# A decoder block with 16,384 experts: first routing result in two halves, row buffers moved, two gathers asked for one stage earlier

## The reference, cut to what matters

```
h = layer_norm(DN_ALPHA * h + merged @ w_out, ln1_g, ln1_b)
q = (h @ w_q).reshape(n, 8, 2, 128)                 # 8 heads, two halves of a key
s = einsum('nhpc,pkc->nhpk', q, sub_keys)           # 128 scores for each half
sv, si = top_k(s, 16)
cand = sv[:, :, 0, :, None] + sv[:, :, 1, None, :]  # 16 x 16 candidates
top_s, pos = top_k(cand, 16)
experts = take_along_axis(cand_idx, pos)            # 16 of 16384 experts for each token and head
gates = softmax(top_s)
act = gelu(einsum('nd,nhkd->nhk', x, u_table[experts])) * gates
out = einsum('nhk,nhkd->nd', act, v_table[experts])
h = layer_norm(DN_ALPHA * h + out, ln2_g, ln2_b)
```

## Time and profile before

| | |
|---|---|
| median of 3 runs | 2435.24 us (2434.62 to 2436.1) |
| the profiled execution, its own time | 2436.59 us |
| its span, first to last instruction | 2434.8 us |
| PE busy | 2155.4 us, 89% |
| DVE busy | 1532.0 us, 63% |
| indirect gathers (queue q0) | 537.01 MB, 52.5% of the 16 DMA engines' span |

### The profile page before, as it was taken

One profiled execution on the slowest core, in us unless ns is written; L12 is line 12 of the kernel. 1 busy time (PEld: TensorE's weight loads), 2 busy tenths in 40 slices (PEclk: granted clock), 3 DMA queues, 4 the chain that ended last, 5 costly groups with the idle time before them and its releaser, 6 DMA issues.

```text
span 2434.8 us, 37735 instructions
## 1 busy us (share of the span) xinstructions
PE 2155.4 (89%) x15287; PEld 1510.0 (62%) x15287; DVE 1532.0 (63%) x2592; ACT 676.3 (28%) x1353; POOL 669.1 (27%) x538
## 2 busy tenths in 40 slices
PE   7999999999999999998988989978887787777776
PEld 6999999999899999887544444433332333222232
DVE  7778888888765454448765576667445544444445
ACT  4555555455344444433111111111111000000000
POOL 1000000000000000003644554555455445444542
PEclk9999999999999999999999999999999999999999
DMA  5433333333366666666999999999999999999997
GB/s 201 130 104 101 105 87 101 104 92 92 102 198 191 184 186 186 210 224 243 416 417 424 420 427 427 427 427 427 427 427 428 426 427 427 427 427 427 427 427 285
DMA packets 346273, 708.19 MB, mean 291 GB/s; under 512 B 13835, under 2 KB 270435, under 8 KB 279779
## 3 DMA queue, kind: packets, MB, share of 16 engines
q0 software_dynamic: 74176, 537.01, 52.5%
q1 hardware_dynamic: 271684, 168.55, 23.4%
q10 hardware_dynamic: 240, 0.22, 0.0%
HBM read 703.63 MB, written 2.10 MB: 290 GB/s over the span
## 4 chain that ended last, share of the span: by engine, by line
DMA 35%; PE 12%; DVE 3%; issue 2%; POOL 1%; DVEq 1%; ACT 0%; POOLq 0%; ACTq 0%
DMA down_rows<-in_v_table,experts 28%; DMA up_rows<-in_u_table,experts 7%; PE bank L1782 7%; PE project L1782 3%; PE bank L1698 1%; DVE up_rows L1898 1%; POOL down_rows L1686 1%; PE bank L1740 0%; PE bank L1725 0%; PE bank L1746 0%; ACT diagonal L1842 0%; DVE one_hot L1348 0%; DVE expert_sides L1354 0%; POOL up_rows L1680 0%; DVE side_index L1327 0%
## 5 line engine op out<-in xcount | busy, mean ns | idle before, releaser
L1898 DVE CUSTOM_DVE_ANT_0 up_rows<-up_rows,h 128x2048 f32<-128x2048 f32 x256 | 585.3, 2292 | 525.9 <-DMA up_rows<-in_u_table,experts 525.8
L1782 PE MATMUL bank<-down_rows,diagonal 128*128 128x512 f32 x1520 | 709.7, 604 | 141.5 <-DMA down_rows<-in_v_table,experts 109.0
L1782 PEld LDWEIGHTS bank<-down_rows,diagonal 128*128 128x128 f32 x1520 | 282.0, 192 | 551.3 <-issue 310.5
L1680 POOL DMA_INDIRECT up_rows<-in_u_table,experts x256 | 286.2, 1118 | 1169.8 <-POOLq L1366 1055.9
L1686 POOL DMA_INDIRECT down_rows<-in_v_table,experts x256 | 374.7, 1464 | 522.5 <-PE bank L1782 508.6
L192 DVE TENSOR_TENSOR w_half_rest<-w_half,w_half_high 128x1024 fp32r<-128x1024 f32 x224 | 271.3, 1219 | 160.1 <-ACT w_half_high L171 159.9
L207 PE MATMUL project<-hT_high,w_half_high 128*128 128x272 f32 (+1 forms) x1152 | 351.5, 305 | 0.4 <-PEq L214 0.3
L207 PE MATMUL project<-hT,w_half_high 128*128 128x272 f32 (+1 forms) x1152 | 329.7, 286 | 0.0
L207 PE MATMUL project<-hT_high,w_half_rest 128*128 128x272 f32 (+1 forms) x1152 | 329.2, 286 | 0.0
L1782 PE MATMUL project<-down_rows,diagonal 128*128 128x512 f32 x512 | 258.8, 629 | 75.6 <-DMA down_rows<-in_v_table,experts 70.6
L171 ACT CAST w_half_high<-w_half 128x1024 fp32r<-128x1024 f32 x224 | 234.7, 1050 | 205.2 <-PE merge_ps L207 121.0
(11 more groups left out here) (376 smaller groups left out, 3043.5 us busy)
## 6 DMA issues: line engine op xcount, KB each, us to landing
w_half<-in_w_in SPq DMA_DIRECT2D x176, 512.0 KB, 3.9
w_half<-in_w_branch_a SPq DMA_DIRECT2D x32, 512.0 KB, 3.8
out_w<-in_w_out SPq DMA_DIRECT2D x16, 1024.0 KB, 5.3
query_w<-in_w_q_peer SPq DMA_DIRECT2D x10, 1024.0 KB, 24.9
w_half<-in_w_branch_b SPq DMA_DIRECT2D x16, 512.0 KB, 3.8
out_w<-in_w_q_peer SPq DMA_DIRECT2D x6, 1024.0 KB, 36.2
up_rows<-in_u_table,experts POOLq DMA_INDIRECT x256, 21.1
down_rows<-in_v_table,experts POOLq DMA_INDIRECT x256, 20.5
```

The source lines that it names most:

```text
L1680: pool.indirect_dma_start(ur[n % RU], None, w["u_table"][0], bass.IndirectOffsetOnAxis(ap=k.idx[:, t, h, j:j + 1], axis=0)).then_inc(s_u[n ...
L1782: mm = nc.tensor.matmul(acc[t][c][:], dg[n % RD][:], vr[n % RV][:, quarter(c)], start=(n == 0), stop=(n == last(t, c)), skip_group_check=True)
L1898: v.tensor_tensor_reduce(ur[n % RU], ur[n % RU], k.h[:, n // (HEADS * TOPK), :], 1.0, 0.0, ALU.mult, ALU.add, dots[:, n:n + 1]).then_inc(s ...
```

## The change

Four things are done at once.

1. In the output stage DVE's order changes: the evacuations and statistics of block n now stand behind the rest bits of quarter 4n + 5; before, they stood behind those of quarter 4n + 6. The loads of head 0's query weights go from g = 4 and 5 to g = 5 and 6.
2. The first routing takes its 16 experts in two halves of 8, and signals `s_ahead` after the first.
3. At the end of the output stage POOL waits for `s_ahead` (and `s_free`, that PE is done with the buffers which lie in the same place) and issues up rows 0 and 1 there. For this the row buffers are allocated earlier: up rows 0, 1, 4, 5 and down rows 0, 1 share the place of six weight buffers of the output stage, up rows 2 and 3 take the place that down rows 3 and 4 had. Before, nine of the eleven buffers started at multiples of 512 bytes and two at bytes 35,520 and 43,712. Now the six start at 130,944 + 8192 i, two at 35,520 and 43,712, and the last three at 180,160, 188,352 and 196,544.
4. After up row 5, POOL issues down rows 0 to 4 in one go; up rows 8 to 15 wait for the second half's `s_idx`.

```diff
+RU, EARLY = 6, 2
...
+    def up_row(self, n):
+        i = n % RU
+        if i in (2, 3):
+            return self.down_or_up[i - 2]
+        return self.rows[:, i if i < 2 else i - 2, :]
...
+def experts(k, h, t, j):
...
+    v.tensor_scalar(k.pij[:, 0, j], k.ti[:, j], 4, None, ALU.logical_shift_right)
+    v.tensor_scalar(k.pij[:, 1, j], k.ti[:, j], 15, None, ALU.bitwise_and)
...
+    return v.tensor_copy(k.idx[:, t, h, j], ex)
...
+    flat, best, rest = cand[:].rearrange("p a b -> p (a b)"), slice(0, 8), slice(8, 16)
+    if halves:
+        v.max(tv[:, best], flat)
+        d()
+        v.max_index(ti[:, best], tv[:, best], flat)
+        v.match_replace(k.cand2[:], tv[:, best], flat, -3.0e38)
+        d()
+        experts(k, h, t, best).then_inc(k.s_ahead, 1)
+        v.max(tv[:, rest], k.cand2[:])
+        d()
+        v.max_index(ti[:, rest], tv[:, rest], k.cand2[:])
+        v.tensor_tensor(k.gates[:, t, h, :], tv[:], tv[:, 0:1].to_broadcast((P, TOPK)), ALU.subtract).then_inc(k.s_shift, 1)
+        d()
+        experts(k, h, t, rest).then_inc(k.s_idx, 1)
+        return
...
-                if g in (4, 5):
-                    k.load_query(sp, w, 0, g - 4)
+                if g in (5, 6):
+                    k.load_query(sp, w, 0, g - 5)
...
-            part(last, 0, 1, 3)
+            part(last, 0, 1, 3).then_inc(k.s_free, 1)
...
-            for g in range(2, 7):
-                rest(g)
             for n in range(NB - 1):
+                for g in range(4 * n + 2, 4 * n + 6):
+                    rest(g)
                 for t in range(TT):
                     evacuate(n, t)
...
-                for g in range(4 * n + 7, min(4 * n + 11, QUARTERS)):
-                    rest(g)
+            for g in range(4 * NB - 2, QUARTERS):
+                rest(g)
             first_tile()
-            route(k, dve, 0, 0)
+            route(k, dve, 0, 0, halves=True)
+
+        @block.gpsimd
+        def _(pool):
+            pool.wait_ge(k.s_ahead, 1)
+            pool.wait_ge(k.s_free, 1)
+            for n in range(EARLY):
+                k.load_up(pool, w, n)
...
-                        if j == 0:
+                        if n == TOPK // 2:
+                            pool.wait_ge(s_idx, 1)
+                        if n and j == 0:
                             pool.wait_ge(s_idx, 2 * h + t + 1)
...
+                        k.load_up(pool, w, n)
+                        if n == RU - 1:
+                            for m in range(RV):
+                                down(m)
```

More of the change, by code:

```diff
@@ L139, in open_routing @@
         self.qT = [self.sb(f"queryT{i}", [P, SEQ]) for i in range(2)]
+        self.rows_at = self.next_at()
+        self.rows = self.sb("rows", [P, 6, D])
+        self.down_or_up = [self.over(f"up_rows{2 + i}", [P, D], self.hT_high_at + 4 * D * i)[:] for i in range(2)]
+        self.s_up, self.s_ahead, self.s_free = [self.sem(f"up_arrived{i}") for i in range(RU)], self.sem("route_idx_first"), self.sem("out_first_free")
         self.s_query_w, self.s_gb = [self.sem(f"query_w{i}") for i in range(3)], self.sem("ln1_gamma_beta")
@@ L1328, in best16, with route @@
     v.drain()
-def route(k, dve, h, t):
+def experts(k, h, t, j):
+    v, d, n = k.nc.vector, k.nc.vector.drain, j.stop - j.start
+    pf, hot, ef, ex = k.pf[:, :, j], k.hot[:, :, j, :], k.ef[:, :, j], k.ex[:, j]
+    v.tensor_scalar(k.pij[:, 0, j], k.ti[:, j], 4, None, ALU.logical_shift_right)
+    v.tensor_scalar(k.pij[:, 1, j], k.ti[:, j], 15, None, ALU.bitwise_and)
+    d()
+    v.tensor_copy(pf, k.pij[:, :, j])
+    d()
+    for i in range(2):
+        v.tensor_tensor(hot[:, i], pf[:, i].rearrange("p (n a) -> p n a", a=1).to_broadcast((P, n, TOPK)),
+                        k.kept[:, C_IOTA:C_IOTA + TOPK].rearrange("p (a n) -> p a n", a=1).to_broadcast((P, n, TOPK)), ALU.is_equal)
+    d()
+    for i in range(2):
+        v.tensor_tensor(hot[:, i], hot[:, i], k.sif[:, i, :].rearrange("p (a n) -> p a n", a=1).to_broadcast((P, n, TOPK)), ALU.mult)
+    d()
+    for i in range(2):
+        v.tensor_reduce(ef[:, i], hot[:, i], AX.X, ALU.add)
+    d()
+    v.scalar_tensor_tensor(out=ex, in0=ef[:, 0], scalar=float(N_KEYS), in1=ef[:, 1], op0=ALU.mult, op1=ALU.add)
+    d()
+    return v.tensor_copy(k.idx[:, t, h, j], ex)
+def route(k, dve, h, t, halves=False):
     v, d = k.nc.vector, k.nc.vector.drain
@@ L1365, in out_stage @@
     QUARTERS = 4 * NB
+    RING = {0: 0, 2: 1, 3: 2}
     with ExitStack() as ctx:
         raw = k.out_raw
-        wh, wt = ([k.out_part(k.hT_high, n) if i == 1 else k.sb(f"out_w{('_high', '_rest')[n]}{i}", [P, QK, 512], ctx=ctx)[:] for i in range(4)]
-                  for n in range(2))
+        wh, wt = ([k.out_part(k.hT_high, n) if i == 1 else k.over(f"out_w{('_high', '_rest')[n]}{i}", [P, QK, 512], k.rows_at + 4 * D * (2 * RING[i] + n))[:]
+                   for i in range(4)] for n in range(2))
         tp, ps = k.bank[0:4], (k.bank[0:2], k.bank[6:8], k.bank[4:6], k.bank[6:8])
@@ L1608, in route_peer_stage @@
         gsum, grec = sb("gate_sum", [P, 1]), sb("gate_rsum", [P, 1])
[L1610 to L1612 removed]
+        ur = [k.up_row(i) for i in range(RU)]
+        vr = [k.rows[:, 4 + i, :] for i in range(2)] + [k.sb(f"down_rows{2 + i}", [P, D], ctx=ctx)[:] for i in range(RV - 2)]
         dg = [sb(f"diagonal{i}", [P, P]) for i in range(RD)]
@@ L1624, in route_peer_stage @@
         s_var1, s_rt1 = k.sem("ln1_second_var"), k.sem("ln1_second_root")
-        s_u = [k.sem(f"up_arrived{i}") for i in range(RU)]
+        s_u = k.s_up
         s_v = [k.sem(f"down_arrived{i}") for i in range(RV)]
@@ L1679, in _ @@
                             pool.wait_ge(s_dot, n - RU + 1)
[L1680 to L1687, removed]
+                        k.load_up(pool, w, n)
+                        if n == RU - 1:
+                            for m in range(RV):
+                                down(m)
+                    for m in due(u)[len(due(u)) * i // UNIT:len(due(u)) * (i + 1) // UNIT]:
+                        if m >= RV:
+                            pool.wait_ge(s_added, m - RV + 1)
+                            down(m)
         @block.tensor
```

24 lines of the change are left out of this document (20 added, 4 removed).

## The result

The changed kernel takes **2446.09 us** (median of 6 runs, 2445.01 to 2446.97), the kernel before took 2436.22 us in the runs beside it (6 runs, 2434.62 to 2437.3). The ratio is 1.0041 [1.0029, 1.0053]: 9.9 us slower, where 12 us faster was forecast, and outside the range of 2420 to 2431. The profiled execution has a span of 2444.4 us (before 2434.8).

A forecast was written before the change was run, and what follows sets the result against it. The prediction took the expert stage's stream of gathers at the DMA engines' full rate as the bound, with PE's then DVE's order ahead of it. 7.8 + 4.5 = 12.3 us off 2435.24 gave 2423, range 2420 to 2431.

The forecast's parts named there:

- Buffers at other addresses ... I take nothing: Expert stage's gathers: moving the row buffers off multiples of 512 bytes costs nothing.
- the rival's 14.1 us: Expert stage's gathers: newly unaligned rows cost 1.4% more each, 14.1 us in all, giving 2437; chance 0.06.
- its estimate, 18 us: Gathers: one more transaction per unaligned descriptor, about 18 us over all rows, a time of 2441 us; not adopted.
- The two early issues ... end at 1115.3 as well, so POOL does not hold the border: End of output stage: POOL's two early issues end about when DVE's routing does (1115.4), so they delay nothing.
- First gather at 1111.9 instead of 1114.50, 2.6 us earlier: End of output stage: routing in halves lets POOL send the first gather early, starting the stream 2.6 us sooner.
- order of the output stage: Output stage: PE's 5.24 us wait goes and quarter 5 runs at the higher clock, 7.8 us off.
- first routing in halves: Border behind the output stage: DVE ends the second half 1.9 us later than before.
- five down rows in one go: Start of expert stage: five down rows fill the gap where the queue ran low, 2.3 us off.
- loads that fill gaps anyway: Early expert stage: gaps already filled with query loads take 0.4 us off the stream's gain, leaving 4.5 us.
- The first rival: Output stage: weights come too late for the earlier PE, so only the stream's 4.5 us remain, 2430.7; chance 0.07.
- a microsecond that the stream starts earlier, or idles less at its start, comes off the end: Expert stage: behind 1191 us only the bytes left count, so any lead at the start shortens the total equally.
- the second rival: Expert stage's start: DVE's 1.9 us and a border held by POOL eat the gain, 7.8 us left, 2427.4; chance 0.10.

The follow-up runs named there:

- run 11: Kernel before with only the output stage's new order and all eleven row buffers at multiples of 256 bytes: 2424.47 us.
- run 12: Changed kernel with all eleven row buffers at multiples of 256, no early gathers, first routing in one piece: 2424.43 us.
- run 3: Kernel before with only the output stage's order changed (DVE's evacuations first, query loads a quarter later): 2426.25 us.
- run 10: Changed kernel with nine row buffers back at multiples of 512, no early gathers, first routing in one piece: 2425.9 us.
- 9: Changed kernel with nine row buffers back at multiples of 512 and no early gather, first routing still in halves: 2428.29 us.
- run 2: Changed kernel with nine of its eleven row buffers back at multiples of 512, halves and two early gathers kept: 2428.74 us.
- 4: Changed kernel with no early gathers, halves and addresses as changed: 2445.54 us.
- run 1: Kernel before with only its nine movable row buffers 64 bytes lower, so all eleven are off multiples of 256: 2453.35 us.
- run 8: Changed kernel with nine row buffers back at multiples of 512 and one early gather instead of two: 2427.29 us.

## Why the prediction was wrong

Two steps failed, and the larger is the one that decided the sign.

**"Buffers at other addresses ... I take nothing"** failed: they cost 17 us. The mechanism and nearly the size stood in the rivals (14.1 us, 2437) and got 0.06. The failed step is the one from two buffers to eleven. The earlier trace rows compare windows of two gathers, read 428 and 425 GB/s, and I read them as no effect. For the two buffers that were off the grid that was right in substance, as far as the steady stream goes: with these two on the grid as well it moves the same 427 GB/s (runs 11 and 12). But what two of eleven cost says little about what eleven cost, since the price is not in proportion (2.473, 2.473, 2.481 and 2.507 us a gather with none, two, five and all off). For the same reason the rival's 14.1 us came near by luck: it was worked out from the 3 GB/s between the two windows as the price of one row of two, and the runs show no such price for those rows. Likewise "427 GB/s throughout, with a fifth of the rows unaligned" was true and spoke for a fifth, not for all. Where the rows hold no arrangement like the new one, and the unknown is multiplied by 410 rows, it belonged into the range and had a claim to far more than 0.06.

The Trainium skill ("DMA: Bandwidth & Descriptors", section "How a descriptor splits into AXI transactions") speaks of the bytes that a transaction fetches from below an unaligned start. The prediction carried that over to the place that is written, since the change moves only the buffers, not the tables; its estimate, 18 us, is close to the 17 measured, and the side was right. The count does not explain the size, though. Worked out by that section's rule, as an estimate, an offset of 128 makes 260 beats for 8 KB and one of 192 makes 262, so the second should cost half as much again, and the runs gave 17.0 and 17.5 us; and two buffers off should cost something as well, and the stream gave nothing. Alignment to 256 bytes as such is what the runs bear out; that the estimate came so near is in part luck.

**"The two early issues ... end at 1115.3 as well, so POOL does not hold the border"** failed. I priced the issuing of the early gathers and not their landing. The border waited for the last byte, 5.96 us in the changed kernel, 2.41 with one gather and 0.32 with none. One early gather came out 1.0 us under none (the ranges overlap) and two 0.5 over it, instead of the gain of **"First gather at 1111.9 instead of 1114.50, 2.6 us earlier"**: that step itself was right (9.8 us earlier, of which 7.2 are the output stage's), only the stream then stood still from 1113 to 1117 until the next request.

The terms of the sum, as put and as measured:

| term | forecast | measured | from |
|---|---|---|---|
| order of the output stage | -7.8 | -9.6 | run 3 |
| first routing in halves | border 1.9 later, taken as covered | +2.4 | run 10 against 9 |
| two early gathers | -2.6 | +0.5 | run 2 against 9; changed kernel against 4 |
| five down rows in one go | -2.3 | 0 | run 12 against 11; -0.35 in run 10 against 3 |
| loads that fill gaps anyway | +0.4 | not measured apart | |
| addresses | 0 | +17.3 | runs 1 and 2 |
| sum | -12.3 | +10.6 | the whole change: +9.9 |

**The output stage** went as written: the wait gone, the quarter at the higher clock. Of the 9.6 us the 7.3 at the first gather are the 7.8 of the sum; the rest behind it was not foreseen. The first rival, weights that come late, did not occur: ACT's cast of quarter 9 began at 1045.62, and PE was done with the last block's first tile at 1087.1, 0.6 us behind the forecast 1086.5.

**Gap filled, nothing won.** "No stretch at 302 GB/s" came true: 8 us from 1132 on read 424 in the changed kernel. But **"a microsecond that the stream starts earlier, or idles less at its start, comes off the end"** was too simple. It holds where DVE's and PE's work moves along with the stream (run 3, and with the opposite sign run 10 against 9), and did not hold where only the stream got ahead (12 against 11, 8 and 9 against 2). Here the second rival, a stream that gains nothing, was right about start and gap. Why the lead is given back at the end is in part argued: the last four down rows are each asked for when PE frees a buffer (POOL waits 3.3 to 3.8 us for it each time, in run 11 as in run 12), the last requests of the two kernels go out within 0.2 us of each other, and the DMA engines are half idle there. No run changed the tail by itself.

## What to carry to other kernels

Price a new address like a new instruction: ask how many transfers land there, and do not scale up from a few buffers that cost nothing. If the trace holds no arrangement like the new one, give the rival its share of the chance (or build the one-line kernel that moves only the buffers). A request sent ahead of a stage's end is only free if the stage's end does not wait for its landing, so look for what drains at a border before moving transfers across it. And being ahead at the start of a saturated stream pays if the engines that ask for the data and use it are ahead too.

## What the runs showed of the hardware

- Gathers of 8 KB to each partition that land off a multiple of 256 bytes bring the core's stream from 427 to 421 or 422 GB/s (all eleven buffers off), or to 426 (the five down buffers off). The time of a gather in the steady part is 2.473 us with none or two of the eleven buffers off, 2.481 with five and 2.507 with all. Offsets of 128 and 192 bytes cost the same, 17.0 and 17.5 us of 2436; 256 costs nothing that the runs can tell (1.0004 [0.9995, 1.0014]). Why the size of the offset does not matter, and why the first two buffers are free, stays open.
- In run 8 the end of the stage opened 0.4 us behind the landing of the gather that POOL had issued inside it (1109.4 and 1109.8), although POOL, in the timeline, has been idle for 4.9 us. That POOL's own drain is what waits was not tried by itself.
- The 5.24 us wait of PE cost 7.3 us at the first gather, because the quarter behind it ran at 0.50 of the clock for a part of its time, and without the wait at 1.00:

```profile
1035.00:1036.00 1.00, 1.00 (x6) 0.81 (x5) 0.00 (x0) 1.00 (x1) 0.00 (x0) 1.00 0.90 293
```
